# Where 14 pieces of another product stand among the steps of an attention stage

## The reference

```
z = q k^T / sqrt(64)                            (strictly causal, s < t)
later[t, s] = sum over s < j < t of log_sigmoid(-z[t, j])
w[t, s] = exp(log_sigmoid(z[t, s]) + later[t, s])
o = w v
```

## Time and profile before

| | us |
|---|---|
| median of 3 runs | 956.43 (951.69, 956.43, 956.82) |
| the profiled execution, its own time | 959.74 |
| its span, from the first to the last instruction | 957.8 |
| PE busy | 931.0 |
| DVE busy | 515.4 |
| ACT busy | 325.8 |
| POOL busy | 216.5 |
| granted clock of TensorE, mean over the span | 0.994 of full speed |

### The profile page before, as it was taken

How to read it: one execution, slowest core, us unless ns; L and a number is a source line. 1 busy time by engine, 2 the same in 40 slices (tenths; PEclk the granted TensorE clock), 3 DMA queues, 4 the chain that set the end, 5 groups by cost and what they waited for, 6 DMA issues and landing times.

```text
span 957.8 us, 13833 instructions
## 1 busy us (share of the span) xinstructions
PE 931.0 (97%) x5547; PEld 782.0 (82%) x5547; DVE 515.4 (54%) x769; ACT 325.8 (34%) x740; POOL 216.5 (23%) x130
## 2 busy tenths in 40 slices
PE   6899999999999999999999999999999899999998
PEld 6788889778877888888888888888888688888886
DVE  4977899698986355444053283133336673334322
ACT  6851222487876221212811101223224630120000
POOL 0003414520010211222243213001110236762000
PEclk9999999999999999999999999999999989999999
DMA  9942503511211211111222536211117653535321
GB/s 314 299 145 77 144 2 110 157 35 29 54 48 45 69 46 44 44 45 55 78 77 99 144 100 176 79 48 52 46 56 255 228 187 103 159 113 178 108 88 66
DMA packets 122697, 100.55 MB, mean 105 GB/s; under 512 B 18087, under 2 KB 104704, under 8 KB 122378
## 3 DMA queue, kind: packets, MB, share of 16 engines
q1 hardware_dynamic: 92330, 76.07, 26.6%
q10 hardware_dynamic: 30304, 23.60, 8.2%
HBM read 73.44 MB, written 24.12 MB: 102 GB/s over the span
## 4 chain that ended last, share of the span: by engine, by line
PE 79%; DVE 10%; DMA 3%; SPq 2%; ACT 2%; issue 2%; POOLq 0%; ACTq 0%; DVEq 0%
PE psum L845 48%; PE psum L272 4%; PE psum L273 4%; PE psum L274 4%; PE psum L281 4%; PE psum L1093 3%; DVE gacc L544 3%; PE psum L1062 2%; DVE sq L720 2%; PE psum L1430 1%; PE psum L1064 1%; SPq L345 1%; DVE ss L722 1%; DMA adag<-in_ada_w 1%; DMA w3raw<-in_w_in 1%
## 5 line engine op out<-in xcount | busy, mean ns | idle before, releaser
L845 PE MATMUL psum<-hhi,w3hl 128*128 128x512 f32 x1120 | 369.1, 398 | 5.2 <-issue 3.5
L845 PEld LDWEIGHTS psum<-hhi,w3hl 128*128 128x128 f32 x1120 | 211.6, 189 | 49.3 <-issue 5.9
L845 PE MATMUL psum<-hlo,w3hl 128*128 128x512 f32 x560 | 219.3, 392 | 0.0
L834 POOL TENSOR_TENSOR w3hl<-w3raw,w3hl 128x1024 fp32r<-128x1024 f32 x43 | 104.8, 2438 | 456.4 <-DVE w3hl L827 456.4
L845 PEld LDWEIGHTS psum<-hlo,w3hl 128*128 128x128 f32 x560 | 106.0, 189 | 19.9
L1192 DVE TENSOR_TENSOR_SCAN stick<-stick,floor 128x1024 f32<-128x1024 f32 (+7 forms) x64 | 89.4, 1444 | 14.2 <-ACT stick L1140 13.8
L845 PE MATMUL psum<-ohi,w3hl 128*128 128x512 f32 x256 | 79.0, 389 | 0.0
L929 ACT COPY zst<-psum 128x512 f32<-128x512 f32 x44 | 25.9, 589 | 132.6 <-PE psum L845 127.5
L680 PE MATMUL psum<-w,hhi 128*128 128x512 f32 x192 | 67.7, 397 | 0.6 <-ACT rows L704 0.6
L827 DVE CAST w3hl<-w3raw 128x1024 fp32r<-128x1024 f32 x43 | 29.5, 687 | 68.0 <-DMA w3raw<-in_w_in 43.2
L845 PEld LDWEIGHTS psum<-ohi,w3hl 128*128 128x128 f32 x256 | 48.1, 188 | 10.0
(11 more groups left out here) (228 smaller groups left out, 1595.2 us busy)
## 6 DMA issues: line engine op xcount, KB each, us to landing
z_scratch<-zst ACTq DMA_DIRECT2D x44, 256.0 KB, 2.4
w3raw<-in_w_in ACTq DMA_DIRECT2D x20, 512.0 KB, 4.3
ada<-in_ada_w SPq DMA_DIRECT2D x16, 512.0 KB, 7.4
w3raw<-in_w_in SPq DMA_DIRECT2D x16, 512.0 KB, 4.1
sg<-z_scratch SPq DMA_DIRECT2D x8, 1024.0 KB, 7.0
xrow<-in_x SPq DMA_DIRECT2D x4, 1024.0 KB, 6.3
w1raw<-in_w_in SPq DMA_DIRECT2D x4, 1024.0 KB, 7.1
adag<-in_ada_w SPq DMA_DIRECT2D x8, 512.0 KB, 4.1
```

The source lines that it names most:

```text
L834: nc.gpsimd.tensor_tensor(lo, w3raw[:], cast(hi), ALU.subtract).then_inc(w3_lo, 1)
L845: t = nc.tensor.matmul(out_, a[:, kt, :], moving[b][:, kt, 512 * half:512 * half + 512], start=(ends[0] and kt == k0 and m == 0), stop=(en ...
```

## The change

The 14 single pieces are put in other steps. Before, they stand in every third step from 17 to 56: 17, 20, 23, 26, 29, 32, 35, 38, 41, 44, 47, 50, 53, 56. After, they stand at the offsets 0, 2, 4, 5 and 6 in the second, third and fourth pair (which begin at steps 16, 32 and 48), four of them in the last: 16, 18, 20, 21, 22, 32, 34, 36, 37, 38, 48, 50, 52, 53. The order of the pieces, the bank, the copies and everything else are the same.

```diff
         FILL_BANK = 6
         fill_at = {-1: 8, 0: 8, 65: 2}
-        fill_at.update({17 + 3 * j: 1 for j in range(PIECES - 2)})
+        fill_at.update({2 * ST * (1 + j // 5) + (0, 2, 4, 5, 6)[j % 5]: 1 for j in range(PIECES - 2)})
```

## The result

The changed kernel takes 960.36 us (median of 11 runs, 956.63 to 963.98) against 955.58 for the kernel before in 11 runs beside it: ratio 1.0054, 95% interval 1.0039 to 1.0069, so about 5.2 us slower (4.8 between the medians). The prediction was 958.6, with 953.2 to 963.4 as its range; direction and range hold, but its sum was +2.2, and the measured loss lies just past the 0.5% that I had given a chance of 0.20.

A forecast was written before the change was run, and what follows sets the result against it. PE was taken to bound the first halves and ACT the turns in the second: 1.95 + 1.30 + 0.75 + 0.80 - 2.59 = +2.2 us on the median 956.43 gave 958.6, range 953.2 to 963.4.

The forecast's parts named there:

- pair 1, first half: PE's steps 0 to 6 of pair 1: three more pieces at 0.65 us each, +1.95 us.
- pair 2, first half, with the bank: PE's steps 0 to 6 of pair 2: two more pieces, +1.30 us, plus a wait for ACT's bank copy, +0.80.
- pair 3, first half: PE's steps 0 to 6 of pair 3: two more pieces, 1.30 us, less a 0.55 wait for the scan, +0.75.
- pair 1, second half: PE's steps 7 to 15 of pair 1: three pieces removed, 15.33 in place of 15.92 us, -0.59.
- pair 2, second half: PE's steps 7 to 15 of pair 2: 15.33 in place of 16.98 us, -1.65, including 0.97 of ACT's work.
- The price of a piece in a first half: Where PE is the bound, one piece of fill costs 0.65 us, with ends 0.30 and 0.70.
- The bank: Step 36 of pair 2: PE waits for ACT's copy of the shared PSUM bank, +0.8 us, ends 0 and 1.5.
- The second halves: PE's steps 7 to 15 of each pair: ACT sets the pace at the turns, removed pieces give back 2.59 us together.
- The clock: Rival: emptied second halves of pairs 1 and 2 lose the clock, 1.7 us per fall; chance 0.17 one, 0.20 both.
- The sum alone: Case in which the added terms hold and no rival acts: 958.6 us, own range 956.5 to 960.5, chance 0.42.
- both falls: Rival case: clock falls in the second halves of pairs 1 and 2, 1.7 us each, 962.0 us; chance 0.20.
- The scans as the bound: Rival: DVE's scans bound the first halves, so the seven pieces cost nothing there, 952.7 us; chance 0.13.

The follow-up runs named there:

- e3_warm: Changed kernel, pieces untouched, with six extra matmuls of 256 columns added in each of steps 13, 29 and 45: 1.0050 against the kernel before, 958.86 us.
- e9_before_warm: Kernel before, pieces untouched, with six extra matmuls added in step 13 alone: 0.9988 against the kernel before, 952.88 us.
- e5_bank: Changed kernel with pair 2's pieces in steps 32, 33, 34, 37 and 38, ending the half tile two steps earlier: 1.0058 against the kernel before.
- e1_tail: Changed kernel with all 14 single pieces moved behind the last attention step, none inside the stage after step 0: 1.0043 against the kernel before, 957.46 us.

## Why the prediction was right, and where its size was off

The terms of the sum can be compared at full clock on both sides, e3_warm (the changed kernel's slots, no fall) against e9_before_warm (the slots before, no fall), in us:

| term | predicted | measured |
|---|---|---|
| pair 1, first half | +1.95 | 17.84 - 16.04 = +1.80 |
| pair 2, first half, with the bank | +1.30 + 0.80 | 17.87 - 15.62 = +2.25 |
| pair 3, first half | +0.75 | 17.12 - 15.72 = +1.40 |
| pair 1, second half | -0.59 | 15.50 - 15.93 = -0.43 |
| pair 2, second half | -1.65 | 15.49 - 16.97 = -1.48 |
| pair 3, second half | -0.35 | 11.73 - 12.44 = -0.71 |
| stage | +2.2 | 130.04 - 127.20 = +2.8 |

**The price of a piece in a first half: right in kind, a little small.** I took 0.65 (0.30 to 0.70); a piece that is on the chain takes 0.71 (e5_bank). Which pieces are on it I had not asked: where the scans lead at the start of a half, a piece ahead of them is free.

**The bank: about right.** The wait is there, 0.59 us of idle PE. Two pieces at 0.71 leave 0.83 of pair 2's growth for it, an estimate, and e5_bank gains 0.3 while it waits 0.48 elsewhere.

**Pair 3's first half: mis-sized.** The piece in step 48 does hide in the wait for a scan, as I said. Here it is at full clock (e3_warm), and PE still waits behind it:

```profile
282.79 0.39 PE L845 MATMUL psum<-hhi,rowsr 128*128 128x512 f32 x1
...
285.10 0.71 PE L281 MATMUL psum<-identr,stickr 128*128 128x128 f32 x6 [0.52 <-DVE stick L1197]
```

What I had wrong is that I left the wait where it was. The second half ahead of it has become shorter, PE comes earlier, and the scan ends 3.19 us into the half in place of 2.50 (285.10 - 281.91 against 283.95 - 281.45). That is 0.69. The other of the two added pieces is on the chain and makes the rest. The +0.71 of the changed kernel's own profile, close to the 0.75 of the sum, is luck: a fall of the clock just before had made PE late.

**The second halves: right.** I took 15.33 at full clock from pair 0; measured with no piece and no extra matmul 15.48 to 15.68 (e5_bank, e1_tail, the changed kernel's pair 0). Pieces there are nearly free up to four.

**The clock: the step that failed.** "The sum alone" was my likeliest case with 0.42, and I gave 0.20 to both falls. Both happened, in two profiles of two, and in pair 1 or pair 2 for twice as long as pair 0 had shown. In the changed kernel's stage they cost 133.70 - 130.04 = 3.7 us (4.1 in the second profile); the kernel before loses 0.7 to its own. With the +2.8 of the slots that makes up the stage's +5.8, and the timed 5.2 (3.7 to 6.6) agrees. But in the times the clock's part is not shown. The kernel with the extra matmuls has the slots without the falls, and at 1.0050 and 1.0053 it is not clearly faster than the changed kernel. For a price of the falls speaks that among the 11 runs of the changed kernel the fastest, 956.63, has the highest granted clock, 0.997, and the slowest, 963.98, the lowest, 0.989; a fall outside the stage counts there too.

The rival's +5.6 (2.2 and two falls at 1.7) was near the 5.2, by parts that offset one another: the slots cost 0.6 more, and the falls 3.7 - 0.7 = 3.0 in place of 3.4, for 10.2 us at half clock in place of 6.8. Its 962.0 and my 958.6 both started from 956.43, the median of 3 runs; in 11 runs it is 955.58, and that lower start brought 958.6 within 1.8 of the result by luck, where the change itself was forecast at less than half. What spoke for the rival was in the earlier trace rows, and I had weighed against it that pair 1's wait was only 0.46: that wait was short because a piece stood in front of it, and the change takes the piece away.

**What follows the stage: not constant.** I let the difference be carried to the end undiminished. What follows took 648.2 us in the profile of the kernel before and 643.5 in that of the changed kernel, so the spans of these two differ by 1.4 us and their stages by 5.8; the late load is in the first of them.

**The scans as the bound: false as a whole, true at the start of two halves.** Its 952.7 did not come. In pair 1 at full clock the scans hold 57.5% of the chain and PE the rest (e1_tail), in pair 3 27.2% (e3_warm). In pair 2 they are not on it (e1_tail). The rule that stood beside this rival, in the Trainium skill, "Perfetto Trace Analysis", section "Identifying the Most-Contended Engine" (take the engine of highest occupancy, TensorE judged by its weight loads), names DVE in both: e1_tail has DVE busy 15.31 of 15.31 us and the weight loads 11.86 in pair 1, 13.22 of 13.91 and 11.88 in pair 2. So this trace agrees for the front part of pair 1 and disagrees for pair 2. The chain of the earlier trace rows was drawn in an execution in which pair 0's fall had hidden pair 1's wait from me.

## What to carry to other kernels

Filler work belongs where the chain of waits runs through other engines, and that is not always where the engine next to it looks busiest: compare the same stretch with and without filler before moving any. When filler leaves a stretch in which TensorE waits for others, price the clock as well; a stretch of the same kernel that has no filler shows what can happen. A wait that a slow clock hides reappears when the clock is restored, so gains of the two don't add.

## What the runs showed of the hardware that I had not expected

A stretch at 1.2 GHz costs less than half of its length where something behind it was waiting anyway: 3.4 us of it in pair 0 were worth 0.76 (1.49 - 0.73), and 10.2 us in the changed kernel's stage 3.7. Eighteen matmuls whose result nobody reads, in three holes, kept the granted clock at 1.00 through the whole stage in both profiles and took no time that the second halves show (15.50 with them, 15.49 without); the timed runs show no gain from them in the changed kernel. And two executions of one kernel, with stages equal to 0.01 us, differed by 5.1 us: all of that arises between 757 and 795 us, with loads that landed late and a fall of the clock behind the wait.
